# Residual update behind three layer norms: four VectorE instructions between later weight tiles in place of four GpSimd instructions behind the border, with the modulation sums spread differently

## The reference

```python
def layer_norm(x, g, b):
    mu = jnp.mean(xf, axis=-1, keepdims=True)
    var = jnp.mean(jnp.square(xf - mu), axis=-1, keepdims=True)
    return (xf - mu) * lax.rsqrt(var + LN_EPS) * g + b

def ada_modulation(c, w, b):
    m = jax.nn.silu(c) @ w + b
    shift, scale, gate = jnp.split(m[:, None, :], 3, axis=-1)
    return shift, scale, 1.0 + gate

for layer in range(DEPTH):
    shift, scale, gate = ada_modulation(c, ada_w[layer, 0], ada_b[layer, 0])
    h = x * (1.0 + scale) + shift
    y = mixer(h)
    x = layer_norm(DN_ALPHA * x + gate * y, ln_g[layer, 0], ln_b[layer, 0])
    shift, scale, gate = ada_modulation(c, ada_w[layer, 1], ada_b[layer, 1])
    h = x * (1.0 + scale) + shift
    y = squared_relu_mlp(h, mlp_w1[layer], mlp_w2[layer])
    x = layer_norm(DN_ALPHA * x + gate * y, ln_g[layer, 1], ln_b[layer, 1])
```

## Time and profile before

| | us |
|---|---|
| median of three runs | 1184.6 |
| lowest and highest run | 1178.47, 1185.64 |
| the profiled execution | 1177.64 |
| its span, first to last instruction | 1175.8 |
| PE busy in the span | 1023.0 (87%) |
| DVE busy | 751.6 (64%) |
| ACT busy | 494.7 (42%) |
| POOL busy | 80.9 (7%) |
| mean granted TensorE clock | 0.925 of full speed |

### The profile page before, as it was taken

One profiled execution on the slowest core, in us unless ns is written; L12 is line 12 of the kernel. 1 busy time (PEld: TensorE's weight loads), 2 busy tenths in 40 slices (PEclk: granted clock), 3 DMA queues, 4 the chain that ended last, 5 costly groups with the idle time before them and its releaser, 6 DMA issues.

```text
span 1175.8 us, 14564 instructions
## 1 busy us (share of the span) xinstructions
PE 1023.0 (87%) x5726; PEld 840.8 (72%) x5726; DVE 751.6 (64%) x1105; ACT 494.7 (42%) x771; POOL 80.9 (7%) x53
## 2 busy tenths in 40 slices
PE   3796788799999978998799999969998988788886
PEld 1474556598989857776599989857886767567664
DVE  2454836787778778554696656576556486885464
ACT  1345232353533342555144444335656255437361
POOL 1000000320000032000061000010000000110000
PEclk9798688899999988999899999989999899989897
DMA  8773252667897865432658865535343155430230
GB/s 317 291 274 114 72 180 71 215 232 258 279 324 284 318 223 194 144 108 72 215 197 237 234 205 189 181 106 178 109 143 99 56 178 179 144 125 19 64 108 36
DMA packets 105303, 204.85 MB, mean 174 GB/s; under 512 B 3834, under 2 KB 38100, under 8 KB 105236
## 3 DMA queue, kind: packets, MB, share of 16 engines
q1 hardware_dynamic: 102180, 193.25, 48.4%
q0 software_dynamic: 3056, 10.67, 3.2%
HBM read 202.76 MB, written 1.15 MB: 173 GB/s over the span
## 4 chain that ended last, share of the span: by engine, by line
PE 60%; DVE 20%; ACT 7%; DMA 7%; issue 5%; SPq 1%; ACTq 0%; DVEq 0%
PE bank L1349 11%; PE bank L1350 11%; PE bank L1351 11%; DVE w_lo L1468 6%; PE bank L1368 5%; PE bank L1370 5%; PE bank L1369 5%; DMA raw<-in_ada_w 5%; PE bank L1427 3%; ACT w_hi L1058 3%; PE bank L1389 2%; DMA raw<-in_mlp_w 2%; PE bank L1314 2%; DVE ht_lo L1473 2%; PE bank L1253 2%
## 5 line engine op out<-in xcount | busy, mean ns | idle before, releaser
L1468 DVE TENSOR_TENSOR w_lo<-raw,w_hi 128x2048 fp32r<-128x2048 f32 (+2 forms) x138 | 319.5, 2330 | 188.8 <-ACT w_hi L1058 188.0
L1058 ACT ACTIVATE w_hi<-raw 128x2048 fp32r<-128x2048 f32 (+2 forms) x138 | 255.2, 1859 | 186.2 <-PE bank L1351 77.1
L1349 PE MATMUL bank<-w_lo,ht_hi 128*128 128x512 f32 (+1 forms) x544 | 225.9, 415 | 45.5 <-DVE w_lo L1468 25.2
L1350 PE MATMUL bank<-w_hi,ht_hi 128*128 128x512 f32 (+1 forms) x544 | 219.2, 403 | 0.0
L1351 PE MATMUL bank<-w_hi,ht_lo 128*128 128x512 f32 (+1 forms) x544 | 218.2, 401 | 0.0
L1349 PEld LDWEIGHTS bank<-w_lo,ht_hi 128*128 128x128 f32 x544 | 108.2, 199 | 72.9 <-issue 38.6
L1368 PE MATMUL bank<-ht_hi,w_lo 128*128 128x256 f32 x512 | 146.7, 286 | 6.6 <-issue 3.8
L1369 PE MATMUL bank<-ht_lo,w_hi 128*128 128x256 f32 x512 | 145.5, 284 | 0.0
L1370 PE MATMUL bank<-ht_hi,w_hi 128*128 128x256 f32 x512 | 145.5, 284 | 0.0
L1351 PEld LDWEIGHTS bank<-w_hi,ht_lo 128*128 128x128 f32 x544 | 107.9, 198 | 23.6
L1350 PEld LDWEIGHTS bank<-w_hi,ht_hi 128*128 128x128 f32 x544 | 108.6, 200 | 21.2 <-issue 0.2
(11 more groups left out here) (185 smaller groups left out, 1213.6 us busy)
## 6 DMA issues: line engine op xcount, KB each, us to landing
raw<-in_mlp_w SPq DMA_DIRECT2D x64, 1024.0 KB, 6.1
raw<-in_ada_w SPq DMA_DIRECT2D x48, 1024.0 KB, 6.5
raw<-in_a_w_in SPq DMA_DIRECT2D x16, 1024.0 KB, 5.3
raw<-in_c_w_in SPq DMA_DIRECT2D x12, 1024.0 KB, 5.6
raw<-in_b_w_in SPq DMA_DIRECT2D x10, 1024.0 KB, 5.0
raw<-in_ple_w_gate SPq DMA_DIRECT2D x8, 1024.0 KB, 5.0
raw<-in_ab_w_in SPq DMA_DIRECT2D x4, 1024.0 KB, 9.3
raw<-in_ab_w_out SPq DMA_DIRECT2D x4, 1024.0 KB, 6.3
```

The lines of the kernel that those rows point to most:

```text
L1058: nc.scalar.activation(split_parts(n)[0], raw_tile(t), ACT.Copy).then_inc(high_done, 1)
L1349: nc.tensor.matmul(dst, a_hi[:, c, rows], lo[:, k, :], start=it["first"] and k == 0, stop=False)
L1350: nc.tensor.matmul(dst, a_hi[:, c, rows], hi[:, k, :], start=False, stop=False)
L1468: nc.vector.tensor_tensor(lo, raw_tile(split[n]), hi.bitcast(F32), ALU.subtract).then_inc(low_done, 1)
```

## The change

The update of `x` at s = 0, 1, 2 becomes a plan item `update` for each token tile, done by DVE in the same two multiplies and adds. At s = 0 and 2 the items stand in `down(0)` behind its third and fourth tile, at s = 1 behind `k[0](0)` of the next mixer. GpSimd no longer computes at these s. The load of `gate_row` now waits for the norm's rows and comes ahead of the loads of `g_row` and `b_row`, which still wait for `resid_done`; `bias_rows` stays behind them. In the MLP of layer 0 the sixteen modulation tiles are spread anew: two in place of four in `down(0)`, two in place of one in `up(2)`, one in place of none in `down(3)`.

```diff
@@ mlp
                     if 2 * n + h in ada:
                         ada_tiles(1)
+                    if g == 0 and n == 1:
+                        add("update", s=2 * layer, t=h)
@@
-            up(1, (3,)), down(0, each), up(2, (3,)), down(1, each), up(3, (1, 3))
+            up(1, (3,)), down(0, (0, 1)), up(2, (1, 3)), down(1, each), up(3, (1, 3))
             columns(2, 0)
             columns(2, 1)
-            down(2, each), down(3)
+            down(2, each), down(3, (0,))
@@ make_plan, mixer of layer 1
     k[0](0)
+    for t in range(T):
+        add("update", s=1, t=t)
     k0 = k[0](1)
@@ gpsimd
             for s in range(N_SUB):
                 if s:
+                    pool.wait_ge(rows_ready, norms[s - 1]["rows"])
+                pool.dma_start(gate_row[:, :], R["ada_b"][s // 2, s % 2, 2 * D:3 * D].partition_broadcast(P)).then_inc(gate_in, 16)
+                if s:
                     pool.wait_ge(resid_done, T * s)
                 pool.dma_start(g_row[:, :], R["ln_g"][s // 2, s % 2].partition_broadcast(P)).then_inc(row_in, 16)
                 pool.dma_start(b_row[:, :], R["ln_b"][s // 2, s % 2].partition_broadcast(P)).then_inc(row_in, 16)
-                pool.dma_start(gate_row[:, :], R["ada_b"][s // 2, s % 2, 2 * D:3 * D].partition_broadcast(P)).then_inc(gate_in, 16)
                 if s == 3:
                     bias_rows()
+                if s < 3:
+                    continue
                 pool.wait_ge(row_in, 32 * (s + 1))
-                for t in range(0 if s < 3 else 1, T):
-                    pool.wait_ge(rows_ready, norms[s]["rows"] - T + t + 1)
-                    if "cut" in norms[s]:
-                        pool.wait_ge(split_done, norms[s]["cut"])
-                    nc.gpsimd.tensor_tensor(x[:, t, :], u[:, t, :], g_row[:, :], ALU.mult).then_inc(pool_step, 1)
...
@@ vector
+                elif kind == "update":
+
+                    t = it["t"]
+                    dve.wait_ge(row_in, 32 * (it["s"] + 1))
+                    link(nc.vector.tensor_tensor(x[:, t, :], u[:, t, :], g_row[:, :], ALU.mult))
+                    nc.vector.tensor_tensor(x[:, t, :], x[:, t, :], b_row[:, :], ALU.add).then_inc(resid_done, 1)
+                    dve.wait_ge(resid_done, T * it["s"] + t + 1)
```

More of the change, by code:

```diff
@@ L1002, in _ @@
                 pool.dma_start(b_row[:, :], R["ln_b"][s // 2, s % 2].partition_broadcast(P)).then_inc(row_in, 16)
-                pool.dma_start(gate_row[:, :], R["ada_b"][s // 2, s % 2, 2 * D:3 * D].partition_broadcast(P)).then_inc(gate_in, 16)
                 if s == 3:
                     bias_rows()
+                if s < 3:
+                    continue
                 pool.wait_ge(row_in, 32 * (s + 1))
-                for t in range(0 if s < 3 else 1, T):
-                    pool.wait_ge(rows_ready, norms[s]["rows"] - T + t + 1)
-                    if "cut" in norms[s]:
-                        pool.wait_ge(split_done, norms[s]["cut"])
-                    nc.gpsimd.tensor_tensor(x[:, t, :], u[:, t, :], g_row[:, :], ALU.mult).then_inc(pool_step, 1)
-                    pool_steps[0] += 1
-                    pool.wait_ge(pool_step, pool_steps[0])
-                    nc.gpsimd.tensor_tensor(x[:, t, :], x[:, t, :], b_row[:, :], ALU.add).then_inc(resid_done, 1)
+                pool.wait_ge(rows_ready, norms[s]["rows"])
+                nc.gpsimd.tensor_tensor(x[:, 1, :], u[:, 1, :], g_row[:, :], ALU.mult).then_inc(pool_step, 1)
+                pool_steps[0] += 1
+                pool.wait_ge(pool_step, pool_steps[0])
+                nc.gpsimd.tensor_tensor(x[:, 1, :], x[:, 1, :], b_row[:, :], ALU.add).then_inc(resid_done, 1)
             for i in range(2):
```

## The result

| | us |
|---|---|
| changed kernel, median of 4 runs | 1201.13 (1198.83 to 1202.55) |
| kernel before, median of 4 runs beside them | 1183.77 (1178.47 to 1185.64) |
| ratio | 1.0157, 95% interval 1.0125 to 1.0188 |
| profiled execution of the changed kernel | 1200.67, span 1198.8, granted clock 0.915 |

The changed kernel is 17.4 us slower. The forecast was 1204.0 us, range 1194 to 1211.

What follows compares the result with a forecast made beforehand. TensorE was taken as the bound, with 60% of the chain of waits, so only its standing still counts. Terms 19.4 + 1.8 - 1.0 - 0.8 = +19.4 us on the median 1184.6 us gave 1204.0 us, range 1194 to 1211.

Steps and rivals of the forecast that it cites:

- The bias table: MLP of layer 1, s = 2: near_bias waits for a 24.0 us load chain, so TensorE stands 19.4 us.
- low end: Bias table at s = 2: shortest chain considered, 16.8 us, giving a TensorE stand of 12.2 us.
- Short chain: Rival at the bias table: small transfers land sooner, +12.2 us in all, 1196.8 us; chance 0.20.
- The clock behind the stand: After TensorE's stand at s = 2, matmuls run at the lower clock for a while, costing 1.8 us once.
- Relief: Borders: faster DVE worth nothing at s = 0, 2, at most 2.96 us at s = 1; rival 23.9 us, chance 0.05.
- forecast of -1.0 us: s = 1: DVE reads the first modulation columns 1.0 us earlier, shortening TensorE's 2.96 us wait.
- MLP of layer 0: Two modulation tiles leave transfer-bound down(0), removing TensorE's longest w_lo wait there: -0.8 us.
- collision of row loads: Rival at s = 0: row loads collide with weight loads, +3.1 in place of -0.8 us, 1207.9 us; chance 0.06.
- Base of the sum: Whole kernel: +19.4 us gives 1197.0 us from the profiled 1177.64 us, 1204.0 us from the median 1184.6 us.

Runs made afterwards that it cites:

- first profile: The kernel before, unchanged, in the profiled execution the prediction was made from: 1177.64 us.
- experiments 3 and 8: Changed kernel with, in 3, the bias_table item two tiles later: 1192.79 us; in 8, both s = 2 updates ahead of down(0): 1188.65 us.
- experiment 5: Kernel before with GpSimd's updates at s = 0, 1, 2 cut to 8 of 1024 columns: 1175.69 us, ratio 0.9939.
- experiment 6: Changed kernel with bias_rows ahead of GpSimd's resid_done wait at s = 3 and the s = 1 updates behind v[0](1): 1177.02 us, ratio 0.9968.
- experiment 4: Changed kernel with bias_rows ahead of GpSimd's resid_done wait and layer 0's modulation tiles spread as in the kernel before: 1183.06 us, ratio 1.0004.
- second and third profile of before: The kernel before, unchanged, profiled twice more: 1182.25 and 1181.77 us.
- first experiment: Changed kernel with the bias_table item of part 1 put behind down(1), eight tiles later: 1179.55 us, ratio 0.9968.
- experiments 2 and 8: Changed kernel with, in 2, bias_rows ahead of GpSimd's resid_done wait: 1179.10 us; in 8, both s = 2 updates ahead of down(0): 1188.65 us.

## Why the prediction was right, step by step

**The bias table.** Right in mechanism, place and size. DVE idle about 24 us: 22.86. A stand of 19.4 us near 668: 18.55. `near_rev` issued near 671 and landed near 682: issued at 665.7 and landed by 678.3 us, since the whole kernel was about 3 us ahead there of the first profile and the first hop 2.3 us shorter than taken. From the end of the second update (655.40) to `near_bias` it is 22.9 us; I had taken 24.0. The hops: to the landing of `rpb_in_rows` 7.0 us (taken 9.25, low end about 4.5), copy, `toeplitz` and first issue 4.7 us (taken 4.8), landing of the second `near_rev` issue 11.2 us (taken 9.9). The first hop was taken 2.3 us too long and the last 1.3 us too short, so that the sum came within 1.1 us is in part luck.

**Short chain.** It did not happen. Behind 670 us little else than `near_rev` moved, as this rival said, and it was slow all the same. By the Trainium skill ("DMA: Bandwidth & Descriptors", Anatomy of one DMA) the chain would be 15.7 us as an estimate, and the trace disagrees, with 22.9 us. Why the last hop was long shows in the windows of the changed kernel. While a weight tile is under way the DMA engines move over 400 GB/s; while only `near_rev` is, they are as busy and move half (the last three columns: clock, DMA share, GB/s):

```profile
662.00:664.00 2.00, 2.00 (x19) 2.00 (x18) 0.00 (x0) 0.00 (x0) 1.34 (x3) 1.00 1.05 408
...
672.00:674.00 2.00, 0.00 (x0) 0.00 (x0) 0.00 (x0) 0.00 (x0) 0.00 (x0) 0.50 1.02 203
674.00:676.00 2.00, 0.00 (x0) 0.00 (x0) 0.00 (x0) 0.00 (x0) 0.00 (x0) 0.50 1.04 211
```

The source rows of `near_rev` are 64 floats, 256 bytes; two issues of 768 KB at 207 GB/s are 7.6 us, most of the median landing of the earlier trace rows. The same page of the Trainium skill (Specifications) says that transfers below 512 bytes miss the line rate, and these rows agree: about half of it.

**The clock behind the stand.** Taken 1.8 us. The MLP grew by 20.7 us, and 18.55 of it is the stand, so 2.1 us; beside the stands of experiments 3 and 8 it is 3.1 and 2.1 us. Right.

**Relief.** Costed at nothing at s = 0 and s = 2: experiment 5 shows it for s = 2, and for s = 0 within 2.6 us. At s = 1 I had said that relief can give 2.96 us at the most, the wait itself. That bound failed: experiment 5 is faster by 4.3 to 10.1 us (the interval), and its stage by 4.2 us, of which 2.7 us are the wait and the rest clock. What brought the clock is open, since experiment 6 has the shorter wait without it. With DVE's update there, the forecast of -1.0 us is neither shown nor refuted: the wait is 2.09 us, as I said, but other profiles of before have 1.46 and 1.20 us, and the stage takes 43.5 to 45.2 us in seven kernels with the update and 44.2 to 44.5 us before.

**MLP of layer 0.** Forecast -0.8 us. The waits for `w_lo` behind `down(0)` went, as experiment 4 shows. The means differ by 1.0 us in that direction, less than single executions spread, so the size is not shown. The collision of row loads (+3.1) did not show: the changed kernel takes 205.3 us there.

**Base of the sum.** Against its own profile the forecast was 1197.0 us, and the profiled execution of the change took 1200.67. Against the second and third profile of before, the difference of the spans is 1198.8 - 1180.3 = 18.5 us, the forecast's 19.4. Going by the median was right. The measured median, 1201.13, is 2.9 us below the forecast of 1204.0.

## What to carry over

When work moves to another engine, list what its completion releases, and put down which instruction waits for the end of that chain: here an update of 2.45 us carried a chain of dependent steps (a load, a copy, a write and a read back) of 23 us. The cure was one of order: put loads that don't need the moved result ahead of the wait in their queue, or use the result later. And profile the kernel before more than once when a difference of 5 us in 1200 is to be placed.

## What the hardware showed unasked

A GpSimd copy of 16x217 took 0.35 us with DVE idle and 2.20 and 1.87 us where a `w_lo` was running on DVE. In the third experiment:

```profile
664.70 2.29 DVE L1473 TENSOR_TENSOR w_lo<-raw,w_hi 128x2048 fp32r<-128x2048 f32 x1 [3.39 <-ACT w_hi L1063]
```

```profile
665.01 2.20 POOL L984 COPY rpb_rows<-rpb_in_rows 16x217 f32<-16x217 f32 x1 [4.11 <-DMA rpb_in_rows<-in_a_rpb]
```

The copy ends at 667.21 us, 0.22 us behind DVE's end at 666.99. In the first experiment the copy ends at 663.58 us and the `w_lo` at 663.36 us, 0.22 us again. In experiments 2 and 8 the copy started while a DVE instruction ran, took 0.61 and 0.38 us, and ended 0.22 and 0.23 us behind it. The Trainium skill ("SBUF — State Buffer", SBUF: two separate sides) calls the port that DVE and GpSimd share a lock held for a whole instruction; all four cases agree.

The same program, from 1060 to 1080 us, was granted a clock of 1.00 once and 0.74 twice. Over the last stage that is 0.93 and 0.91, and 5.5 to 5.7 us of a span of 1180.
